# Another layout for the pairs' activations, a merged last read, and SwiGLU at once in pairs 10 and 11

## The chip, the cores and the metric

One core of one Trainium2 chip runs the kernel. The metric is the device time of that core in microseconds. Five engines share an on-chip memory (SBUF): TensorE (PE; its weight loads are shown as PEld), VectorE (DVE), ScalarE (ACT), GpSimd (POOL) and SyncE (SP), which issues the transfers. TensorE writes into eight banks of 128x512 floats (PSUM).

## What is computed

A transformer block over 512 tokens of width 2048, all in float32: a projection, two attentions, gates and an output projection, cross attention, and then the part of interest here, which the reference writes as

```python
def swiglu(h, w_gu, w_down):
    g, u = jnp.split(h @ w_gu, 2, axis=-1)
    return (jax.nn.silu(g) * u) @ w_down
...
hf = rmsnorm(x, norm_ffn_g[l])
x = x + swiglu(hf, w_gu[l], w_down[l])
```

with 5632 hidden features, that is 44 tiles of 128. A final norm follows.

## The kernel before

Activations are kept transposed: 16 tiles (k) of 128 features by 512 tokens. For accuracy each float is split in two parts, a high one (rounded to the type that TensorE multiplies) and the low rest, and a product is high x high + high x low + low x high. ScalarE makes the high part of a piece of weights (`convert`, `mix_convert`, lines 597 and 946), VectorE subtracts it from the raw one to make the low part (`units`, `mix_low`, lines 1093 and 1580), TensorE uses both. Weights stream in pieces called units.

Of the 44 hidden tiles two (DIRECT) are computed plainly, by `panel` in `ffn_first` and behind it (lines 2159 to 2237). The other 42 make 21 **pairs**, each with a gate product and an up product of two tiles: 42 groups g, and group 2p-2 is the gate of pair p, 2p-1 its up. A group is computed with seven block products for eight (Strassen's scheme in Winograd's form, `PRODUCTS`, line 132): blocks of the features' halves by the tokens' halves. Three of the products ("b") read the activations themselves (blocks B11, B21 and B22), four ("t") read sums prepared in `t_both`. GpSimd makes the sums of the weights (lines 564 to 571). A group has four units c; in each of them every product gets four matmuls: two wide ones, high weights by low and high activations beside each other (128x512, line 2175), and two narrow ones, low weights by high activations (128x256, line 2178). Each group leaves seven banks: product 0 in one of two acc banks, by turns, the others in six that all groups share.

VectorE reads a group's banks in `read_products` (line 1597) while TensorE works on the group's last unit and on the next group's first. The reading is told by semaphore of products 0, 2, 4 and 5 (`TOLD`) and of the unit's end, and frees banks in four steps (`READ_STEPS`, `FREED_BY`), for which TensorE waits before the next group's products 1, 3, 5 and 6. Every addition waits for the one before. Between two readings VectorE makes four low parts. ScalarE can make the high part of unit n once unit n-3 is done (line 951).

For pairs 1 and 2 (`INLINE`) SwiGLU is done at once: VectorE scales the gate product by the norm's factor `rstd`, ScalarE takes the sigmoid, VectorE multiplies twice, and after the up product once more; the result is stored to `gate_t`. For the other pairs gate and up product are stored to memory, and are fetched, scaled and multiplied in the down stage. There the rows of w_down run in `ORDER`, with 11 groups of four hidden tiles. The first of them needs the two inline pairs, for nothing is left to do on them but the split.

The **seam** is the passage from pairs to down stage. SyncE fetches the first weights of the down stage, then per unit a part of x, and once, at c == 1, both pairs of tiles of `hidden_in(0)` (lines 487 to 498). ScalarE and VectorE split them, VectorE before it reads the last group (lines 1716 to 1729). TensorE starts on the down stage when both are split; its two acc banks come free when VectorE has added the first ones to x (`add_out`, line 1453; `down`, line 1669). SBUF space is shared: `over` (fetched tiles, and two of four places for the raw weights of pairs, `mix_raw`) and `act_both` lie on the same bytes.

## Time and profile before

| | |
|---|---|
| median of 3 runs | 2774.85 us (2771.26 to 2776.34) |
| profiled execution, its own time | 2777.86 us |
| its span, first to last instruction | 2776.1 us |
| mean granted clock of TensorE | 0.994 |
| busy: PE / PEld / DVE / ACT / POOL | 98% / 82% / 63% / 37% / 27% |
| stage of the pairs | 1413.6 to 2269.4 us |
| down stage, with its end | 2269.6 to 2776 us |

The rows show one execution. PE is busy from a matmul's start to its modelled end, and matmuls overlap, so the time that TensorE loses is read from the distance of starts and from the waits. "L1585" is line 1585 of the kernel. The arrow "<-" in a wait names what released it. A wide matmul of two separate runs of 256 and one of a single run of 512 have the same shape in a row, 128x512.

### The profile page before, as it was taken

How to read it: one execution, taken by the hardware profiler on the slowest of the kernel's cores; microseconds unless marked ns; L12 is line 12 of the kernel's file. 1: busy time of each engine (PE TensorE's matmuls, PEld its weight loads, DVE VectorE, ACT ScalarE, POOL GpSimd, SP SyncE). 2: the span in 40 equal slices, each digit the busy share in tenths (PEclk: the TensorE clock that was granted, in tenths of full speed). 3: DMA queues.
4: the chain of work that ended last, by engine and by line, in shares of the span. 5: the costliest groups of instructions: out<-in, count | busy, mean ns of one | idle time of the engine just before them, and what ended most of it. 6: DMA issues, size and time to landing. Idle time of an engine off the chain costs nothing.

```text
span 2776.1 us, 35075 instructions
## 1 busy us (share of the span) xinstructions
PE 2720.1 (98%) x13710; PEld 2285.9 (82%) x13710; DVE 1742.1 (63%) x1904; ACT 1018.1 (37%) x1134; POOL 742.4 (27%) x642
## 2 busy tenths in 40 slices
PE   9999999999999999999998999999999999999997
PEld 7888888888788888887777888888888878888886
DVE  6677643345643343674677767777777767777786
ACT  6545532224642231243643333333333332222224
POOL 0000000000000003420366566665656532222120
PEclk9999999999999999999999999999999999999999
DMA  6222233232223334333333343434343464434432
GB/s 239 73 91 68 68 103 98 91 99 85 79 82 97 98 119 165 95 117 104 129 112 104 127 138 128 137 123 143 122 142 124 138 231 132 154 132 153 158 123 84
DMA packets 125890, 333.30 MB, mean 120 GB/s; under 512 B 10320, under 2 KB 57424, under 8 KB 125136
## 3 DMA queue, kind: packets, MB, share of 16 engines
q1 hardware_dynamic: 119296, 309.37, 34.4%
q10 hardware_dynamic: 6480, 22.35, 2.0%
q8 instruction: 79, 1.29, 0.2%
q14 instruction: 35, 0.29, 0.0%
HBM read 301.27 MB, written 30.41 MB: 119 GB/s over the span
## 4 chain that ended last, share of the span: by engine, by line
PE 80%; DVE 14%; ACT 2%; issue 1%; DMA 1%; POOL 1%; SPq 0%; DVEq 0%; ACTq 0%
PE acc L1803 14%; PE acc L1805 14%; PE acc L1804 14%; PE ps L2175 9%; PE acc L1830 6%; PE acc L1831 6%; PE acc L1832 6%; PE ps L2178 5%; PE acc L2175 2%; DVE w_lo L1585 2%; DVE cg L1612 2%; DVE cg L1613 2%; DVE cu L1613 2%; DVE cu L1612 2%; DVE wm_lo L1585 1%
## 5 line engine op out<-in xcount | busy, mean ns | idle before, releaser
L1098 DVE TENSOR_TENSOR w_lo<-raw,w_hi 128x1024 fp32r<-128x1024 f32 x328 | 476.6, 1457 | 282.9 <-ACT w_hi L607 282.3
L1803 PE MATMUL acc<-act_both,w_hi 128*128 128x512 f32 (+1 forms) x1536 | 590.9, 385 | 1.3 <-DVE sq_sum L1490 1.0
L1805 PE MATMUL acc<-act_both,w_lo 128*128 128x512 f32 (+1 forms) x1536 | 584.9, 381 | 0.0
L1804 PE MATMUL acc<-act_both,w_hi 128*128 128x512 f32 (+1 forms) x1536 | 584.7, 381 | 0.0
L607 ACT ACTIVATE w_hi<-raw 128x1024 fp32r<-128x1024 f32 x328 | 344.6, 1055 | 565.6 <-PE acc L1805 339.2
L1803 PEld LDWEIGHTS acc<-act_both,w_hi 128*128 128x128 f32 x1536 | 289.2, 188 | 57.0 <-DVE sq_sum L1490 1.5
L1805 PEld LDWEIGHTS acc<-act_both,w_lo 128*128 128x128 f32 x1536 | 289.1, 188 | 55.6
L1804 PEld LDWEIGHTS acc<-act_both,w_hi 128*128 128x128 f32 x1536 | 289.3, 188 | 54.6 <-issue 0.7
L2175 PE MATMUL ps<-t_both,w_hi 128*128 128x512 f32 x896 | 282.6, 397 | 0.1
L541 POOL MEMSET mem_stat<- 128x256 f32 x1 | 0.3, 312 | 1049.2 <-DMA mem<-mem_t 1049.2
L1830 PE MATMUL acc<-act_both,w_hi 128*128 128x512 f32 x672 | 263.5, 392 | 4.3 <-DVE x L1453 4.0
L1831 PE MATMUL acc<-act_both,w_hi 128*128 128x512 f32 x672 | 262.4, 390 | 0.0
L1832 PE MATMUL acc<-act_both,w_lo 128*128 128x512 f32 x672 | 262.1, 390 | 0.0
L1453 DVE TENSOR_TENSOR x<-x,acc 128x512 f32<-128x512 f32 (+1 forms) x216 | 147.5, 683 | 140.3 <-PE acc L1832 86.7
L2178 PEld LDWEIGHTS ps<-t_both,w_lo 128*128 128x128 f32 x896 | 168.9, 188 | 40.0
L1585 DVE TENSOR_TENSOR w_lo<-raw,w_hi 128x1792 fp32r<-128x1792 f32 x56 | 121.4, 2168 | 87.9 <-ACT w_hi L952 87.0
L2178 PE MATMUL ps<-t_both,w_lo 128*128 128x256 f32 x896 | 176.5, 278 | 0.0
L952 ACT ACTIVATE w_hi<-raw 128x1792 fp32r<-128x1792 f32 x56 | 95.4, 1703 | 192.8 <-PE ps L2178 179.1
L952 ACT ACTIVATE w_hi<-over 128x1792 fp32r<-128x1792 f32 x56 | 95.6, 1706 | 172.9 <-PE ps L2178 162.1
L569 POOL TENSOR_TENSOR over<-over 128x512 f32<-128x512 f32 x84 | 155.1, 1846 | 6.6
L1830 PEld LDWEIGHTS acc<-act_both,w_hi 128*128 128x128 f32 x672 | 126.4, 188 | 34.7 <-DVE w_lo L1098 4.1
L1832 PEld LDWEIGHTS acc<-act_both,w_lo 128*128 128x128 f32 x672 | 126.6, 188 | 26.6
(300 smaller groups left out, 4718.9 us busy)
## 6 DMA issues: line engine op xcount, KB each, us to landing
raw<-w_stream SPq DMA_DIRECT2D x412, 512.0 KB, 3.6
over<-w_stream SPq DMA_DIRECT2D x84, 512.0 KB, 4.7
gate_t<-cg ACTq DMA_DIRECT2D x22, 512.0 KB, 2.6
over<-gate_t SPq DMA_DIRECT2D x22, 512.0 KB, 5.4
up_t<-cu ACTq DMA_DIRECT2D x20, 512.0 KB, 2.6
over<-up_t SPq DMA_DIRECT2D x20, 512.0 KB, 6.2
x<-x_t SPq DMA_DIRECT2D x16, 512.0 KB, 8.9
x_tokens<-x_n SPq DMA_DIRECT2D x4, 1024.0 KB, 15.4
```

The lines of the kernel that those rows point to most:

```text
L607: nc.scalar.activation(w_hi[:, s, :], raw[:, s, :], ACT.Copy).then_inc(hi_done, 1)
L952: nc.scalar.activation(mix_half(True, i), mix_raw(i)[:, 1:8, :], ACT.Copy).then_inc(hi_done, 1)
L1098: nc.vector.tensor_tensor(w_lo[:, s, :], raw[:, s, :], f(w_hi[:, s, :]), ALU.subtract)\
L1585: nc.vector.tensor_tensor(mix_half(False, i), mix_raw(i)[:, 1:8, :], f(mix_half(True, i)), ALU.subtract).then_inc(lo_done, 1)
L1803: nc.tensor.matmul(dst, wh, ah, start=start and k == 0, stop=False)
L1804: nc.tensor.matmul(dst, wh, al, start=False, stop=False)
L1805: last = nc.tensor.matmul(dst, wl, ah, start=False, stop=stop and k == UK - 1)
L1830: nc.tensor.matmul(dst[n], wh, ah, start=k == 0, stop=False)
L1831: nc.tensor.matmul(dst[n], wh, al, start=False, stop=False)
L1832: last = nc.tensor.matmul(dst[n], wl, ah, start=False, stop=k == GROUP - 1)
L2175: nc.tensor.matmul(dst, hi[:, w_block, P * j:P * (j + 1)], src[:, :, ks.start + 2 * c + j, toks], start=c == 0 and j == 0, stop=False)
L2178: last = nc.tensor.matmul(dst[:, SH:S], lo[:, w_block, P * j:P * (j + 1)], src[:, 1, ks.start + 2 * c + j, toks], start=False, stop=c == 3 ...
```

## The change

- The activations for the direct panels and the pairs lie in `act_mix`, by tile k, half of the tokens, low or high part, 256 tokens. The low and the high part of one block stand beside each other, and a wide matmul of a "b" product reads 512 floats in one run. A direct panel reads the two halves of a tile's tokens, 256 each, from two places. The "t" products are unchanged. Hidden tiles of the down stage lie in `late`, by tile, then low or high; `over` likewise, so two fetched tiles are no longer in one run.
- The six shared banks are numbered in a row. `read_products` reads products 5 and 6 together, with two additions over two banks once the unit is done; three steps and three tellings remain.
- `INLINE` is 10, 11 and `ORDER` starts with them. In these pairs the third multiplication of the gate (by `rstd`) is moved behind the up product, and the multiplications there lie behind one low part each. The numbers of the waits for stored products follow from `UPS_STORED`. ScalarE's order in the pairs is as it was.
- The seam: the first fetched pair of tiles is asked for at c == 0, the second at c == 1, each with a semaphore of its own. ScalarE's high part of the second pair of tiles moves behind a high part of weights; VectorE's split of the first moves ahead of a low part, and the low part between the last reading and the first addition to x moves behind that addition.

The diff, cut to its core (left out: declarations, the passing of `x_low` a view, renamings from act to late, the waits' numbers on ScalarE):

```diff
@@ -132,13 +132,14 @@
-READ_STEPS = 4
-FREED_BY = {1: 1, 3: 2, 5: 3, 6: 4}
-TOLD = (0, 2, 4, 5)
...
-INLINE = 2
-ORDER = [*range(1, MIXES + 1), 0]
+READ_STEPS = 3
+FREED_BY = {1: 1, 3: 2, 5: 3}
+TOLD = (0, 2, 4)
...
+INLINE = 10, 11
+ORDER = [*INLINE, *(p for p in range(1, MIXES + 1) if p not in INLINE), 0]
+UPS_STORED = [1 + sum(q not in INLINE for q in range(1, p + 1)) for p in range(MIXES + 1)]
@@ -193,10 +194,16 @@
         with ExitStack() as a:
-            over = sb("over", [P, 2, KT, S], F32, a)
+            over = sb("over", [P, KT, 2, S], F32, a)
+        with ExitStack() as a:
+            act_mix = sb("act_mix", [P, KT, 2, 2, SH], F32R, a)
+        with ExitStack() as a:
+            late = sb("late", [P, KT, 2, S], F32R, a)
         act_both = sb("act_both", [P, 2, KT, S], F32R)
         act_lo, act_hi = (act_both[:, n, :, :] for n in range(2))
-        over_lo, over_hi = (over[:, n, :, :] for n in range(2))
+        over_lo, over_hi = (over[:, :, n, :] for n in range(2))
+        mix_lo, mix_hi = (act_mix[:, :, :, n, :] for n in range(2))
+        late_lo, late_hi = (late[:, :, n, :] for n in range(2))
         raw = sb("raw", [P, RING, UK * P], F32)
@@ -266,7 +273,8 @@
         acc = [ctx.enter_context(nc.psum_tensor(f"acc{n}", [P, S], F32)) for n in range(2)]
-        ps = [ctx.enter_context(nc.psum_tensor(f"ps{n}", [P, 3 * S], F32)) for n in range(2)]
+        both_ps = ctx.enter_context(nc.psum_tensor("ps", [P, 6 * S], F32))
+        ps = [both_ps[:, 3 * S * n:3 * S * (n + 1)] for n in range(2)]
@@ -351,14 +362,17 @@
         def hid_tile(slot, k):
-            return act_tile(UK + GROUP * slot + k)
...
+            return late_hi[:, UK + GROUP * slot + k, :], late_lo[:, UK + GROUP * slot + k, :]
...
+        def halves(tile):
+            return tile.rearrange("p (t c) -> p t c", t=2)
...
             if n % 4 >= 2:
-                return (over_lo, over_hi)[n % 4 - 2][:, 0:UK, SH:S]
+                return over[:, 0:UK, 1, SH * (n % 4 - 2):SH * (n % 4 - 1)]
             return raw[:, 2 * (n % 4):2 * (n % 4) + 2, :].rearrange("p r (b c) -> p (r b) c", b=4)
@@ -378,11 +392,10 @@
                 return acc[n][:]
-            t, b = ((0, 0), (0, 1), (1, 0), (1, 1), (0, 2), (1, 2))[i - 1]
-            return ps[t][:, S * b:S * (b + 1)]
+            return both_ps[:, S * (i - 1):S * i]
         def two_banks(t, h):
-            return ps[t][:, 0:2 * S].rearrange("p (a s) -> p a s", a=2)[:, :, SH * h:SH * (h + 1)]
+            return both_ps[:, 2 * S * t:2 * S * (t + 1)].rearrange("p (a s) -> p a s", a=2)[:, :, SH * h:SH * (h + 1)]
@@ -466,14 +479,14 @@
-            def hidden_in(g):
...
-                for b in range(0, GROUP, 2):
+            def hidden_in(g, parts=range(0, GROUP, 2)):
...
+                for b in parts:
                     p = ORDER[2 * g + b // 2]
                     sp.wait_ge(gate_stored, 16 * (p + 1))
-                    sp.dma_start(over_lo[:, hid_part(g % 2, b), :], gate_t[p, :, :, :]).then_inc(hid_in[g % 2], 16)
+                    sp.dma_start(over_lo[:, hid_part(g % 2, b), :], gate_t[p, :, :, :]).then_inc(hid_in[g % 2] if g else hid_in_first[b // 2], 16)
                     if g:
-                        sp.wait_ge(up_stored, 16 * (p - INLINE + 1 if p else 1))
+                        sp.wait_ge(up_stored, 16 * UPS_STORED[p])
                         sp.dma_start(over_hi[:, hid_part(g % 2, b), :], up_t[p, :, :, :]).then_inc(hid_in[g % 2], 16)
@@ -489,8 +502,8 @@
                 sp.wait_ge(unit_done, U_DOWN - 3 + c)
-                if c == 1:
-                    hidden_in(0)
+                if c < 2:
+                    hidden_in(0, [2 * c])
                 x_in_again(c)
@@ -926,7 +939,9 @@
                 for m in (2 * n, 2 * n + 1):
-                    x_high(act_hi[:, m, :], m, G_FFN)
+                    read_out()
+                    nc.scalar.activation(mix_hi[:, m, :, :], halves(x[:, m, :]), ACT.Copy,
+                                         scale=par[:, G_FFN + m:G_FFN + m + 1]).then_inc(h_hi, 1)
                     if m > 1:
@@ -1017,17 +1032,18 @@
                     mix_convert()
-                    convert(1)
-                    act.wait_ge(hid_in[0], 32)
                     for b in range(0, GROUP, 2):
-                        nc.scalar.activation(act_hi[:, hid_part(0, b), :], over_lo[:, hid_part(0, b), :], ACT.Copy)\
+                        if b:
+                            convert(1)
+                        act.wait_ge(hid_in_first[b // 2], 16)
+                        nc.scalar.activation(late_hi[:, hid_part(0, b), :], over_lo[:, hid_part(0, b), :], ACT.Copy)\
                             .then_inc(hid_hi, 1)
...
                 if inline:
-                    act.wait_ge(hid_made, p)
+                    act.wait_ge(hid_made, INLINE.index(p) + 1)
                     store_gate(p)
@@ -1622,10 +1638,8 @@
                 between()
-                dve.wait_ge(products_done, len(TOLD) * g + 4)
-                added(out[:, 1, :], out[:, 1, :], lambda h: half(5, h), freed)
                 dve.wait_ge(unit_done, U_MIX + 4 * (g + 1))
-                added(out[:, 2, :], out[:, 2, :], lambda h: half(6, h), freed)
+                added(out[:, 1:3, :], out[:, 1:3, :], lambda h: two_banks(2, h), freed)
@@ -1700,32 +1714,33 @@
             rstd_of(4, rstd, S)
             mix_low(4)
             for p in range(1, MIXES + 1):
-                inline, last = p <= INLINE, p == MIXES
+                inline, last = p in INLINE, p == MIXES
                 dve.wait_ge(gate_stored, 16 * p)
                 read_products(2 * p - 2, cg)
                 mix_low()
                 if inline:
-                    dve.wait_ge(up_stored, 16)
+                    dve.wait_ge(up_stored, 16 * UPS_STORED[p - 1])
                     nc.vector.tensor_tensor(cg[:], cg[:], both, ALU.mult).then_inc(gate_scaled, 1)
                 mix_low()
                 if inline:
-                    dve.wait_ge(sig_made, p)
+                    dve.wait_ge(sig_made, INLINE.index(p) + 1)
                     link(nc.vector.tensor_tensor(cg[:], cg[:], cu[:], ALU.mult))
-                    link(nc.vector.tensor_tensor(cg[:], cg[:], both, ALU.mult))
                 mix_low()
                 if last:
+                    hidden_low(0, 0)
                     units()
-                    hidden_low(0, 0)
                     hidden_low(0, 2)
                 else:
                     mix_low()
-                dve.wait_ge(up_stored, 16 * (max(0, p - INLINE - 1) + 1))
+                dve.wait_ge(up_stored, 16 * UPS_STORED[p - 1])
                 read_products(2 * p - 1, cu, units if last else lambda: None)
                 if inline:
-                    nc.vector.tensor_tensor(cg[:], cg[:], cu[:], ALU.mult).then_inc(hid_made, 1)
-                if last:
-                    units()
-                else:
+                    mix_low()
+                    link(nc.vector.tensor_tensor(cg[:], cg[:], cu[:], ALU.mult))
+                    mix_low()
+                    nc.vector.tensor_tensor(cg[:], cg[:], both, ALU.mult).then_inc(hid_made, 1)
+                    mix_low(2)
+                elif not last:
                     mix_low(4)
             unit.add(MIX_UNITS * MIXES)
@@ -1748,9 +1763,9 @@
                 for n in range(KT // 2):
-                    down(2 * n, first=first, between=lambda: next_group(n))
...
-            arrived = Tally(32), Tally()
+                    down(2 * n, first=first, between=units if first and n == 0 else lambda: next_group(n))
...
+            arrived = Tally(), Tally()
             per_group = [(converted, KT), (unit, KT), (out_no, 2 * KT), (half, KT), (hid, GROUP), (arrived[0], 64),
@@ -2170,14 +2185,16 @@
                         pe.wait_ge(products_read, READ_STEPS * (g - 1) + FREED_BY[at])
-                    src = act_both if kind == "b" else t_both
+                    if kind == "b":
+                        src = [act_mix[:, ks.start + 2 * c + j, toks.start // SH, :, :] for j in range(2)]
+                    else:
+                        src = [t_both[:, :, ks.start + 2 * c + j, toks] for j in range(2)]
                     for j in range(2):
-                        nc.tensor.matmul(dst, hi[:, w_block, P * j:P * (j + 1)], src[:, :, ks.start + 2 * c + j, toks],
-                                         start=c == 0 and j == 0, stop=False)
+                        nc.tensor.matmul(dst, hi[:, w_block, P * j:P * (j + 1)], src[j], start=c == 0 and j == 0,
+                                         stop=False)
                     for j in range(2):
-                        last = nc.tensor.matmul(dst[:, SH:S], lo[:, w_block, P * j:P * (j + 1)],
-                                                src[:, 1, ks.start + 2 * c + j, toks], start=False,
-                                                stop=c == 3 and j == 1)
+                        last = nc.tensor.matmul(dst[:, SH:S], lo[:, w_block, P * j:P * (j + 1)], src[j][:, 1, :],
+                                                start=False, stop=c == 3 and j == 1)
                     if c == 3 and at in TOLD:
```

## Rows read from the trace of the kernel before

**Rows 1.** Busy times of a stretch: start:end; length, PE, PEld, DVE, ACT, POOL, clock, DMA.

```profile
1413.40:2269.50 856.10, 836.22 (x4706) 721.46 (x4704) 613.57 (x671) 289.65 (x173) 539.88 (x498) 0.99 0.41 132
```

**Rows 2.** Timeline of TensorE, steady group: start us, us, what, count.

```profile
1699.71 0.63 PE L2175 MATMUL acc<-act_both,wm_hi 128*128 128x512 f32 x2
...
1700.41 0.63 PE L2175 MATMUL ps<-act_both,wm_hi 128*128 128x512 f32 x2
...
1704.59 0.63 PE L2175 MATMUL acc<-act_both,w_hi 128*128 128x512 f32 x2
```

**Rows 3.** Waits of weight loads, 1532.9 to 2253 us: total, times, longest.

```profile
PEld acc L2175 <- DVE w_lo L1585: 9.7, 24, 0.7
PEld acc L2175 <- DVE wm_lo L1585: 5.1, 12, 0.9
```

**Rows 4.** Waits of matmuls, 1413.5 to 1532.9 us: total, times, longest.

```profile
PE acc L2175 <- DVE wm_lo L1585: 6.1, 3, 2.8
PE acc L2175 <- DVE w_lo L1585: 6.0, 4, 3.4
```

**Rows 5.** Busy times of a stretch behind a long wait, with its granted clock.

```profile
1511.30:1518.10 6.80, 5.40 (x17) 4.63 (x18) 5.22 (x3) 1.04 (x1) 1.69 (x2) 0.50 0.62 215
```

**Rows 6.** Timeline of VectorE, one reading of a steady group.

```profile
2007.08 0.69 DVE L1612 TENSOR_TENSOR cg<-ps,cg 128x512 f32<-128x512 f32 x1 [0.51 <-PE ps L2178]
2007.81 0.69 DVE L1613 TENSOR_TENSOR cg<-ps,cg 128x512 f32<-128x512 f32 x1
...
2010.90 0.42 DVE L1612 TENSOR_TENSOR cg<-ps,cg 128x256 f32<-128x256 f32 x1
...
2012.73 2.02 DVE L1585 TENSOR_TENSOR wm_lo<-raw,wm_hi 128x1792 fp32r<-128x1792 f32 x1
```

**Rows 7.** Timeline of TensorE at the unit that follows that reading.

```profile
2014.24 0.40 PE L2178 MATMUL ps<-t_both,w_lo 128*128 128x256 f32 x2
2014.81 0.74 PE L2175 MATMUL acc<-act_both,wm_hi 128*128 128x512 f32 x2 [0.17 <-DVE wm_lo L1585]
```

**Rows 8.** Timeline of VectorE and ScalarE, gate product of pair 2.

```profile
1484.85 2.02 DVE L1585 TENSOR_TENSOR w_lo<-raw,w_hi 128x1792 fp32r<-128x1792 f32 x1
...
1486.80 1.22 DVE L1709 TENSOR_TENSOR cg<-cg,rstd 128x1024 f32<-128x1024 f32 x1
...
1488.05 1.06 ACT L1013 ACTIVATE cu<-cg 128x1024 f32<-128x1024 f32 x1 [9.24 <-DVE cg L1709]
...
1490.73 2.41 DVE L1585 TENSOR_TENSOR w_lo<-over,w_hi 128x1792 fp32r<-128x1792 f32 x1 [2.72 <-ACT w_hi L952]
...
1493.07 2.31 DVE L1713 TENSOR_TENSOR cg<-cg,cu 128x1024 f32<-128x1024 f32 x1
```

**Rows 9.** Timeline of TensorE, down stage: whole tiles, then the halves of its end.

```profile
2725.93 0.39 PE L1830 MATMUL acc<-act_both,w_hi 128*128 128x512 f32 x1
...
2727.97 0.39 PE L1830 MATMUL acc<-act_both,w_hi 128*128 128x512 f32 x1
...
2739.79 0.28 PE L2227 MATMUL acc<-act_both,w_hi 128*128 128x256 f32 x1
...
2740.03 0.28 PE L2229 MATMUL acc<-act_both,w_lo 128*128 128x256 f32 x1
```

**Rows 10.** Timeline of SyncE queue, ScalarE and VectorE at the seam.

```profile
2259.74 1.49 SPq L474 DMA_DIRECT2D over<-gate_t  x2
...
2266.11 2.01 ACT L1023 ACTIVATE act_both<-over 128x1024 fp32r<-128x1024 f32 x2 [0.36 <-DMA over<-gate_t]
...
2269.47 0.42 DVE L1617 COPY cu<-acc 128x256 f32<-128x256 f32 x1
...
2277.17 1.23 DVE L1098 TENSOR_TENSOR w_lo<-raw,w_hi 128x1024 fp32r<-128x1024 f32 x1
```

**Rows 11.** Timeline of TensorE at the seam.

```profile
2275.00 0.39 PE L1832 MATMUL acc<-act_both,w_lo 128*128 128x512 f32 x1
2279.14 0.64 PE L1830 MATMUL acc<-act_both,w_hi 128*128 128x512 f32 x1 [3.75 <-DVE x L1453]
```

34 lines of the change are left out of this document (18 added, 16 removed).

## Prediction

> **What bounds the kernel now.** The page comes first: TensorE is busy for 98% of the span and VectorE for 63%, so a change can pay in two ways only, by making TensorE's own work shorter or by closing its gaps. Next I cut the span by stage. The stage of the pairs (lines 2164 to 2191, 168 units of 28 matmuls) lasts 856 us and TensorE is busy for 836 of them [rows 1], but "busy" counts a matmul from start to modelled end and these overlap, so idle time is read better from the starts. With no wait, one unit begins 4.88 us after the last (1699.71 to 1704.59), one product 0.70 us after the last [rows 2]. 168 x 4.877 = 819.3 us. The stage takes 855.8 from first start to last, so 36.5 us of it are waits and their after-effects. The rest of the prediction is mainly about these.
>
> They fall in two heaps. In the 36 steady groups the weight loads wait 9.7 + 5.1 = 14.8 us, always for the low halves of the weights (line 1585), 0.41 a group [rows 3]. In the first five groups, where SwiGLU is done at once for pairs 1 and 2, TensorE's matmuls wait 12.1 us in seven places [rows 4], and two stretches at half clock follow the long ones, 3.4 us and 6.8 us at 0.50; the second is shown [rows 5]. From the unit starts, the groups with pairs 1 and 2 lose 18.7 us against 4.877 a unit, of which 4.3 is time at the lower clock.
>
> **Part 1, the reading.** For one group VectorE reads seven products (lines 1616 to 1628) and only then makes the next low half. In a steady group the reading ends at 2012.73; its last four additions of 128x256 take 2012.73 - 2010.90 = 1.83 us, 0.46 each, while one addition over two banks comes 2007.81 - 2007.08 = 0.73 after the other [rows 6]. The change makes two of the second kind out of the four: 1.46 us for 1.83, and the low half begins 0.38 us sooner, with 0.69 us of work each and the same link between them. It removes one wait (fourth "products_done") and keeps the wait for the whole unit; that one is met long before, since the group's last unit, 4.88 us long, starts at 2004.72 and ends near 2009.6, and the two additions begin at 2010.90 [rows 6]. The next low half ends at 2014.75, the load of its weights starts after it, and the matmul comes at 2014.81; without a wait the load would have come just after the previous unit's last matmul (second of the two that begin at 2014.24, so 2014.36) [rows 6, 7]. Hence 0.45 us lost now. With 0.38 less, 0.07 stays, and about 0.02 more since TensorE gets a little quicker (part 3): 0.09. For 37 groups (all but the first and the four with SwiGLU in them) 37 x 0.36 = 13.3 us. Who waits for the merged step: TensorE's product 5 of the next group writes a bank that is freed by it, and comes 5 x 0.70 = 3.5 us into its unit, at 2013.1; the step ends at 2012.35. No new wait, with 0.7 us to spare. Should it cost what four took, the gain is 0; should the whole wait vanish, 37 x 0.45 = 16.6.
>
> **Part 2, SwiGLU in pairs 10 and 11 for pairs 1 and 2.** What is removed at the start: 18.7 us. What stays there: in group 0 the reading starts late (VectorE had to catch up with the first weights), and its first unit after the reading waits 1.27 us for matmuls, 1.78 by the starts, of which 0.38 goes by part 1; I leave 1.5 us. What is added in the middle is read from pair 2, the one nearest to a steady start. Gate product: low half (1484.85), times rstd (1486.80, 1.22 us), sigmoid on ScalarE (1488.05, 1.06), then ScalarE's next high half, and only then VectorE's next low half at 1490.73, which took 2.41 [rows 8]. This queue is not changed: ScalarE still waits with its high half behind the sigmoid. So one wait stays, 1.1 in matmul idle and 1.4 by the starts; part 1 takes 0.38 of it, the pair lands a little later against a unit without loss: 1.0 to 1.7 us, I take 1.3. What is gone: the third multiplication ahead of the third low half (1.65 us, which cost the wait of 0.8), and the one ahead of the low half after the odd reading, which cost 3.4 us and the half clock behind it. They lie now behind two low halves each. VectorE has room: a group needs 6.3 us of reading and 4 x 2.0 of low halves out of 19.5, so 5.2 are free, against two multiplications of 1.2 (alone) to 2.3 us (2.31 at 1493.07, beside GpSimd) [rows 8]. After the odd reading ScalarE's last two high halves wait for the product, as they did; by the order it is there some 14 us into the group and the low half at 18.3, needed at 19.5; if both multiplications take 2.3 it is late by 1 us. So 2 x 1.3 = 2.6 us, bounds 2 and 8. Sum of part 2: 18.7 - 1.5 - 2.6 = 14.6; the two groups of each new pair keep 0.09 of part 1 as well, -0.4: 14.2.
>
> The Trainium skill ("SBUF — State Buffer", Who interferes with whom) says that a VectorE instruction with two SBUF inputs contends with GpSimd's reads. The trace agrees: 2.31 us for a multiplication beside GpSimd's work, 1.22 without.
>
> **Part 3, the layout.** A wide matmul on the pairs reads two runs of 256 that lie far apart, two of them span 0.63 us, so 0.63 - 0.40 = 0.233 from start to start [rows 2]; on one run of 512 it is (2727.97 - 2725.93)/9 = 0.227 [rows 9]. Three of seven products change: 168 x 3 = 504 of them, two wide matmuls each. A whole product takes 0.697. Made of contiguous prices, 2 x 0.227 + 2 x 0.120 (narrow ones in a row, 2739.79 to 2740.03 [rows 9]) = 0.694: 3 ns less, 1.5 us in all. If instead the narrow ones keep what they have now, it is 12 ns less, 6.3 us. I take 2.0, nearer to the first end, since each product is as long as its four matmuls at their own prices. Against it: the four direct panels (192 wide matmuls of line 1803 to 1805) now read two runs: 192 x 6 ns = 1.2 us more. Net gain 0.8. ScalarE, VectorE and the transfers touch the same number of elements in other strides; I cost this at nothing, because these engines are waited for at the places named here only, and price a few ns a matmul among the rivals.
>
> The skill ("SBUF — State Buffer", Door 1: The DMA port swizzle) has it that only a step beyond a 16-byte line costs; by that rule one jump in 512 elements is free, and the layout brings nothing (total 0.8 us worse than mine).
>
> **Part 4, the seam.** Now: both gate tiles of the first down group are fetched at 2259.74, ScalarE has them at 2266.11, VectorE splits both (1.15 each) and starts reading the last group at 2269.47, though its products were there from about 2265.3; the reading with one low half in it ends at 2277.17, another low half (1.15) follows, then the first addition to x (0.68); TensorE, with nothing free to write to, stands from 2275.2 to 2279.14, and then 3.4 us at half clock come [rows 10, 11]. After: tiles 0 and 1 are fetched a unit earlier, their split (done by about 2263.5) leaves the path; then low half (2265.8), second split, reading at 2268.2: 1.3 us sooner. It takes 4.7 + 1.2 (low half) + 1.45 = 7.35 for 7.7, and the second low half lies behind the addition to x: addition done at 2276.2, TensorE resumes at 2276.4. Stall 1.6 in place of 3.9 us, and no half clock after so short a one (behind the waits of 1.3 and 2.5 us the clock stayed at its upper level, behind those of 2.8 and 3.4 [rows 4] and this one it fell): 2.3 + 1.5 + 0.4 at the first down matmuls (they waited for the second split) = 4.2 us. Bounds 2.5 (half clock stays) and 5.
>
> **Sum.** 13.3 + 14.2 + 0.8 + 4.2 = 32.5 us. Profiled execution: 2777.9 - 32.5 = 2745.4; it is 3.0 above the median of the runs, 2774.85, so the time is 2742.4, said as 2742.5.
>
> **Rivals.** (a) The lower weights stay late: the merged additions over two banks save nothing, or the load that begins late costs a refill anyway (about 0.1 us after each wait is seen in the first matmul, 0.74 for two instead of 0.63 [rows 2, 7]). Then the 13.3 us stay: 2756. For it: 0.09 us of margin is computed from a difference of 0.07. Against: the chain of the reading is link by link and leaves no slack elsewhere. (b) SwiGLU costs in the middle what it cost at the start, because the loss comes from ScalarE's order, which stays: 2 x 9 - 2.6 = 15 us more, less the clock part if no stall is as long as those: 2753 to 2757. For it: the same wait of 1.4 us is kept. Against: two of the three long waits sat behind multiplications that are moved. (c) Contiguous reading pays fully, 2738. (d) Slower than before: the two halves lying together make TensorE's read, not its array, the limit for the 1008 wide matmuls of the b products, or for those of the down stage, say through other engines working in the same tile. Each ns on 1008 matmuls is 1.0 us. It decides from 33 ns a matmul (0.260 in place of 0.227); at 40 ns the time is 2782. Against: the largest effect of form in the trace is 6 ns. (e) The change does not do what it says: all of layout and merging bring nothing, and only the moved SwiGLU and the seam are left, 2757, as in (a).
>
> **Chances.** Forecast 0.64, (a) with (e) 0.13, (b) 0.12, (c) 0.08, (d) 0.03. Range: from 2733 (forecast with layout and refill at their best ends: 5 + 3 us, seam 1) to 2758 (a or b alone); both together, 2771, lie outside. About 0.2% (5.5 us) is what a measurement of this kernel can tell from no change: faster by more 0.95 (all but (d), less 0.02 for (a) and (b) at once and at their worst), within 0.02, slower by more 0.03.
>
> **What would show it.** Steady groups: weight loads wait under 0.15 us a group for line 1585's successor and units at 4.87 throughout; waits of the first two pairs down to one of 1 to 1.5 us; one stall of 1 to 1.7 us in each of groups 18 and 20 and no half clock near them; the b products shorter than the t products by 3 ns (or 12); the seam's stall near 1.6 us at full clock. Wrong would be: a half-clock stretch in the middle, waits of TensorE for products_read, b products no shorter, or a slower down stage (matmuls there more than 0.227 apart).

## The result, and the profile after

The changed kernel takes 2757.4 us (median of 4 runs, 2755.5 to 2758.8) where the kernel before took 2775.6 beside it: ratio 0.9937, 95% interval 0.9920 to 0.9954. That is 0.6% faster, 14.9 us more than the predicted 2742.5 and at the upper edge of the range (2758). The profiled execution took 2757.35 us (span 2755.6) against 2777.86: 20.5 us less, where the sum said 32.5. (The other 3 us of the miss are the distance by which the profiled execution of before lay above its median, which I took off; that of after lies on it.)

The page's busy times of after:

```profile
PE 2708.8 (98%) x13710; PEld 2282.3 (83%) x13710; DVE 1740.2 (63%) x1820; ACT 1019.7 (37%) x1134; POOL 768.4 (28%) x642
```

The stretch of the pairs, from the first to the last matmul, answering [rows 1]:

```profile
1413.30:2247.20 833.90, 824.86 (x4706) 718.11 (x4705) 615.05 (x591) 289.59 (x173) 564.85 (x498) 1.00 0.42 135
```

The waits of matmuls at the start (1413.3 to 1510 us), answering [rows 4]:

```profile
PE acc L2193 <- DVE wm_lo L1601: 0.7, 1, 0.7
PE acc L2193 <- DVE w_lo L1601: 0.5, 1, 0.5
```

The waits of weight loads between 1510 and 1770 us and, second line, between 1885 and 2250 us, answering [rows 3]:

```profile
PEld acc L2193 <- DVE wm_lo L1601: 0.5, 1, 0.5
...
PEld acc L2193 <- DVE w_lo L1601: 0.4, 1, 0.4
```

The stage of the pairs is 22 us shorter and its granted clock is 1.00. The waits of weight loads in the steady groups, 14.8 us before, are 0.9 in the two stretches shown; those of the first five groups, 12.1 us, are 1.2, with no stretch at the lower clock behind them. (These views list no wait under 0.15 us; by the starts of the units 0.07 us a steady group is left.) What is new stands in the middle, pairs 10 and 11 (waits of matmuls, 1770 to 1885 us):

```profile
PE acc L2193 <- DVE w_lo L1601: 3.9, 3, 2.4
PE acc L2193 <- DVE wm_lo L1601: 3.5, 3, 1.3
```

By the starts of the units, as in the prediction (excess over 4.877 us a unit; "start" is the first five groups, "middle" groups 18 to 23, "rest" the other 31), the two profiled executions compare so:

| | before | predicted change | measured change | after |
|---|---|---|---|---|
| first pair matmul at | 1413.63 | +1.2 | -0.25 | 1413.38 |
| units' own time, 168 x 4.877 | 819.3 | -2.0 | 0.0 | 819.3 |
| start | 18.7 | -16.8 | -16.6 | 2.2 |
| middle | 2.65 | +0.5 | +6.6 | 9.2 |
| rest | 14.95 | -11.2 | -11.8 | 3.1 |
| behind the last pair matmul | 506.9 | -4.2 | +1.6 | 508.5 |
| sum | | -32.5 | -20.5 | |

(The predicted -27.5 of parts 1 and 2 is shared out over start, middle and rest by its own steps: 0.36 a group, 18.7 to 1.5, and 2.6 for the two new pairs.) Three lines missed: the middle by 6, the seam by 6, the layout's units by 2. The experiments are about these three, and about which part of the change earned what.

### The profile page after: what moved, and what is told of

Same layout as the page of the kernel before. It is cut to its first block, busy times and chain, and to the rows that moved or that the text cites. A ratio compares the mean times of both kernels' runs of the same rounds, so it can differ in the third digit from the quotient of the medians.

```text
span 2755.6 us, 34949 instructions
## 1 busy us (share of the span) xinstructions
PE 2708.8 (98%) x13710; PEld 2282.3 (83%) x13710; DVE 1740.2 (63%) x1820; ACT 1019.7 (37%) x1134; POOL 768.4 (28%) x642
## 4 chain that ended last, share of the span: by engine, by line
PE 88%; DVE 6%; ACT 2%; issue 2%; DMA 1%; POOL 1%; SPq 0%; DVEq 0%; ACTq 0%
PE ps L2193 14%; PE acc L1818 14%; PE acc L1820 14%; PE acc L1819 14%; PE ps L2196 7%; PE acc L1845 5%; PE acc L1846 5%; PE acc L1847 5%; PE acc L2193 3%; PE acc L2196 1%; DVE w_lo L1601 1%; DMA x_tokens<-x_n 1%; PE ps L1887 1%; PE ps L1876 1%; DVE cg L1629 1%
## 5 line engine op out<-in xcount | busy, mean ns | idle before, releaser
L1818 PE MATMUL acc<-act_both,w_hi 128*128 128x512 f32 (+1 forms) x1472 | 565.4, 384 | 1.2 <-DVE sq_sum L1506 1.0
L1820 PE MATMUL acc<-act_both,w_lo 128*128 128x512 f32 (+1 forms) x1472 | 559.9, 380 | 0.0
L1819 PE MATMUL acc<-act_both,w_hi 128*128 128x512 f32 (+1 forms) x1472 | 559.5, 380 | 0.0
L1818 PEld LDWEIGHTS acc<-act_both,w_hi 128*128 128x128 f32 x1472 | 277.1, 188 | 54.4 <-DVE sq_sum L1506 1.5
L1820 PEld LDWEIGHTS acc<-act_both,w_lo 128*128 128x128 f32 x1472 | 276.9, 188 | 53.1
L1819 PEld LDWEIGHTS acc<-act_both,w_hi 128*128 128x128 f32 x1472 | 277.2, 188 | 51.7 <-issue 0.5
L1845 PE MATMUL acc<-late,w_hi 128*128 128x512 f32 x672 | 263.5, 392 | 5.8 <-DVE x L1469 5.8
L1846 PE MATMUL acc<-late,w_hi 128*128 128x512 f32 x672 | 262.4, 390 | 0.0
L1847 PE MATMUL acc<-late,w_lo 128*128 128x512 f32 x672 | 262.1, 390 | 0.0
L1845 PEld LDWEIGHTS acc<-late,w_hi 128*128 128x128 f32 x672 | 126.4, 188 | 36.6 <-DVE w_lo L1114 4.2
L1847 PEld LDWEIGHTS acc<-late,w_lo 128*128 128x128 f32 x672 | 126.6, 188 | 26.6
```

The costliest lines, as they stand in the source:

```text
L1818: nc.tensor.matmul(dst, wh, ah, start=start and k == 0, stop=False)
L1819: nc.tensor.matmul(dst, wh, al, start=False, stop=False)
L1820: last = nc.tensor.matmul(dst, wl, ah, start=False, stop=stop and k == UK - 1)
L1845: nc.tensor.matmul(dst[n], wh, ah, start=k == 0, stop=False)
L1846: nc.tensor.matmul(dst[n], wh, al, start=False, stop=False)
L1847: last = nc.tensor.matmul(dst[n], wl, ah, start=False, stop=k == GROUP - 1)
```

## Experiments

All were timed beside the kernel before. "Pairs" is the time from the first to the last pair matmul, "end" what lies behind it, both of the profiled execution. One trace's small differences need care: e9 and e11 below run the same instructions in the middle and lose 3.9 and 2.1 us there, and among e8, e9, e10 and e12, which are the same from the seam on, the end takes 505.9 to 506.6 us.

**e1, the layout alone** (kernel before, with `act_mix`, `late`, the new `over` and what reads them)

```diff
-            over = sb("over", [P, 2, KT, S], F32, a)
+            over = sb("over", [P, KT, 2, S], F32, a)
...
+            act_mix = sb("act_mix", [P, KT, 2, 2, SH], F32R, a)
...
+            late = sb("late", [P, KT, 2, S], F32R, a)
...
```

> Only the layout of act_mix, late and over changes. Prediction's theory (contiguous reads are quicker): products of the b kind 3 ns shorter, the direct panels' matmuls 6 ns longer, in all 0.8 us faster. Theory after the first trace (a wide matmul's 0.233 comes from narrow ones beside it, not from two runs): every product stays 0.697 us, panels stay 0.227 a matmul, stage of the pairs 855 to 856 us; fetches into over go in 2 KB pieces, 1.9 us each for 1.3, but the seam has slack for that: 0 to +1.5 us in all.

2777.3 us, ratio 1.0011 (1.0002 to 1.0021): a little slower, not faster, and 1 us more than the second theory allowed. A unit without a wait takes 4.877 us as before. The pairs are 2.9 us shorter than before, but 2.9 of that is the start, which in this execution had one stretch of half clock fewer; the end is 3.0 us longer.

**e2, the merged reading alone**

```diff
-READ_STEPS = 4
+READ_STEPS = 3
...
-                added(out[:, 1, :], out[:, 1, :], lambda h: half(5, h), freed)
-                added(out[:, 2, :], out[:, 2, :], lambda h: half(6, h), freed)
+                added(out[:, 1:3, :], out[:, 1:3, :], lambda h: two_banks(2, h), freed)
```

> Only the last two products are read together. My theory: the low half after each reading comes 0.38 us sooner, weight loads wait 0.07 a group for 0.44, in all 41 groups 14 to 16 us faster, stage of the pairs about 840 us. Rival (the refill of the weights is paid anyway): 0.1 or more stays besides, 10 us or less.

2756.4 us, ratio 0.9936 (0.9919 to 0.9952): this one edit gives all that the whole change gives. Pairs 835.2 us, 20.4 less: 12.5 in the rest, 2.2 in the middle (together 14.7 for 37 groups, 0.40 each), and 5.6 at the start, where in this execution no half clock follows the long waits. The waits of its matmuls in the first five groups, SwiGLU still in pairs 1 and 2, and of its weight loads in all later groups:

```profile
PE acc L2173 <- DVE w_lo L1585: 5.3, 4, 2.6
PE acc L2173 <- DVE wm_lo L1585: 4.9, 3, 2.8
```

```profile
PEld acc L2173 <- DVE wm_lo L1585: 0.3, 1, 0.3
```

The waits at the start are still 10.2 us, with longest ones of 2.6 and 2.8; the excess is 13.1 us instead of 18.7.

**e3, SwiGLU moved to pairs 10 and 11 alone** (the new `INLINE`, `ORDER`, `UPS_STORED` and the order of the multiplications)

> Only pairs 10 and 11 instead of 1 and 2 get SwiGLU at once, with the multiplications in their new places. Prediction's theory: the start gains 17 us, the middle costs 2 x 1.3: 14 us faster. Theory after the first trace: the middle costs about 9 to 11 us, since VectorE comes late to the next reading and its low half after it runs beside GpSimd (2.6 to 2.9 us for 2.0): 4 to 8 us faster, no half clock in the pairs.

2769.1 us, ratio 0.9981 (0.9971 to 0.9991). The start falls from 18.7 to 3.6 us, the middle rises from 2.65 to 9.8: half of the gain is given back. The second theory holds (4 to 8 us, no half clock), the prediction's 14 us does not.

**e4, the seam's order alone**

```diff
-                if c == 1:
-                    hidden_in(0)
+                if c < 2:
+                    hidden_in(0, [2 * c])
...
-                    units()
                     hidden_low(0, 0)
+                    units()
                     hidden_low(0, 2)
```

> Only the seam's order changes, layout as before (4 KB pieces). Theory of the 2 KB pieces: the weights of the down stage's fifth unit land about 11 us after the last pair's matmul, not 13.4; the stall before the third unit is about 1.7 us for 4.0; in all 1.5 to 4.5 us faster than before. Rival (the order itself moves the wait from the first to the second place whatever the pieces): stall of 4 us there and half clock behind it, +1 us or no change.

2774.3 us, ratio 0.9998 (0.9988 to 1.0007): nothing. The long stall is gone, and with it the half clock, but TensorE now stands three times (its matmuls that waited at the seam):

```profile
2275.51 0.47 PE L1829 MATMUL acc<-act_both,w_hi 128*128 128x512 f32 x1 [1.68 <-DVE x L1454]
2282.36 0.47 PE L1829 MATMUL acc<-act_both,w_hi 128*128 128x512 f32 x1 [1.16 <-DVE x L1454]
2289.96 0.47 PE L1829 MATMUL acc<-act_both,w_hi 128*128 128x512 f32 x1 [1.90 <-DVE x L1454]
```

The first is the 1.6 us that was predicted. The two others are new: each time VectorE is held up by a low part of weights that has to be fetched first. Of the expected theory the landing of the weights holds (11.1 us) and the gain doesn't; of the rival only "no change" does, for there is no stall of 4 us and no half clock.

**e5, the changed kernel with the down stage's weights asked for first**

```diff
-            hidden_in(1)
             late_weights(4)
-            for c in range(4, 8):
-                x_in_again(c)
+            hidden_in(1, [0])
+            late_weights(5)
+            hidden_in(1, [2])
+            late_weights(6)
+            x_in_again(4)
+            late_weights(7)
+            x_in_again(5)
...
```

> The changed kernel, but in the seam SyncE asks for the weights of the down stage's units 4 to 7 ahead of or between the fetches of hidden tiles and x, not behind them. Theory (the seam is bound by the transfer queue, in the order in which it is asked): the stall of 4.2 us before the third unit and the half clock behind it go, the time behind the last pair's matmul falls from 508.5 to 502 to 504 us, 5 to 6 us faster than the changed kernel. Rival (VectorE's order of low parts and additions is what binds): no more than 1 us.

2754.6 us, ratio 0.9926 (0.9909 to 0.9942), the intervals overlap with those of the changed kernel (2757.4). The weights of unit 4 come in time, and the stall of 3.84 us in matmul idle becomes two of 1.7, behind the first one, which is as it was:

```profile
2261.51 0.50 PE L1851 MATMUL acc<-late,w_hi 128*128 128x512 f32 x1 [1.73 <-DVE x L1475]
2266.25 0.47 PE L1851 MATMUL acc<-late,w_hi 128*128 128x512 f32 x1 [1.73 <-DVE x L1475]
```

Now VectorE waits for the hidden tiles of the next group, which were moved back (idle for 3.82 us until they land). The end stays at 508.5 us, so the theory's 502 to 504 is refuted: bringing the weights forward is not enough.

**e6, the changed kernel with ScalarE's next high half ahead of the sigmoid**

```diff
-                mix_convert()
+                mix_convert(2)
                 if inline:
                     act.wait_ge(gate_scaled, INLINE.index(p) + 1)
                     nc.scalar.activation(cu[:], cg[:], ACT.Sigmoid).then_inc(sig_made, 1)
-                mix_convert()
```

> The changed kernel, but ScalarE makes the second high half of an inline pair ahead of the sigmoid, not behind it. Theory (the wait of 1.35 us in the gate group is ScalarE's order, and VectorE's lateness in the next groups starts from it too): the two waits of 1.3 us and part of the four behind them go, pairs 10 and 11 cost 3 to 5 us in place of 9.2. Rival (the loss is VectorE's own load of multiplications beside GpSimd, whatever ScalarE does): 7 us or more stay.

2752.2 us, ratio 0.9919 (0.9903 to 0.9936), 5.2 below the changed kernel (the intervals overlap); the middle falls from 9.2 to 4.6 us. VectorE and ScalarE in the first gate product of e6:

```profile
1791.95 2.02 DVE L1600 TENSOR_TENSOR wm_lo<-over,wm_hi 128x1792 fp32r<-128x1792 f32 x1
```

```profile
1792.06 1.06 ACT L1028 ACTIVATE cu<-cg 128x1024 f32<-128x1024 f32 x1 [3.98 <-DVE cg L1722]
```

The low half starts straight behind the multiplication (1790.81, 1.22 us), while the sigmoid runs.

**e7, wide matmuls first, narrow ones behind them** (changed kernel; in the first three units of each group, since the fourth has to end product by product. The expectation below speaks of the two middle units; what ran reorders one unit more, c = 0, and that one decides the time.)

```diff
-                    for j in range(2):
-                        last = nc.tensor.matmul(dst[:, SH:S], lo[...], src[j][:, 1, :], ...)
+                    if c < 3:
+                        srcs[at] = (w_block, dst, src)
...
+                for at, args in srcs.items():
+                    last = narrow(at, *args)
```

> The changed kernel, but in the two middle units of each group all 14 wide matmuls come first, then all 14 narrow ones. Theory (0.233 and 0.115 are the prices of wide and narrow matmuls beside each other, 0.227 and 0.120 those in a row of one width, whatever the runs): wide matmuls of those units 0.227 apart, narrow 0.120, a unit 4.86 us for 4.877, 1 to 2 us faster. Rival (the pairs' operands or addresses cost it): wide matmuls stay 0.233.

2774.3 us, ratio 0.9998 (0.9989 to 1.0008). The timeline of TensorE in a unit of e7, and its waits for VectorE's reading between 1533 and 2240 us:

```profile
1704.67 0.62 PE L2201 MATMUL ps<-act_mix,w_hi 128*128 128x512 f32 x2
1705.13 1.53 PE L2201 MATMUL ps<-t_both,w_hi 128*128 128x512 f32 x6
1706.49 0.62 PE L2201 MATMUL ps<-act_mix,w_hi 128*128 128x512 f32 x2
...
1707.87 0.88 PE L2188 MATMUL ps<-t_both,w_lo 128*128 128x256 f32 x6
1708.59 0.40 PE L2188 MATMUL ps<-act_mix,w_lo 128*128 128x256 f32 x2
```

```profile
PE ps L2201 <- DVE cu L1629: 5.2, 19, 0.4
PE ps L2201 <- DVE cg L1629: 5.0, 18, 0.6
```

Six wide matmuls on `t_both`, two distant runs of 256 each, take 1706.49 - 1705.13 = 1.36 us, 0.227 apiece; the two on `act_mix`, one run of 512, take 0.46, 0.23 each, the same within the rows' hundredths. The narrow ones take 0.72 / 6 = 0.120. So the distances of 0.233 and 0.115 in [rows 2] belong to wide and narrow matmuls by turns, not to the layout: 7 x 4 matmuls take 4.873 us in one order and 4.877 in the other. The time is lost at c = 0: product 5's bank is written 2.3 us into the unit there instead of 3.5 (1706.49 against 1704.20), before the merged step has freed it, and the unit takes 5.48 us. So the expected distances are there, and the expected gain of 1 to 2 us is not.

**e8, all of the change but the layout**

> The changed kernel without its layout: merged read, moved SwiGLU and the seam's order only. Theory (the layout gives TensorE nothing and costs the seam transfers of 2 KB pieces): the pairs take 833 to 834 us as in the changed kernel, and the time behind their last matmul falls by 2 us, fetches into over take 1.3 us each for 1.8; 2 us faster than the changed kernel. Prediction's theory: 1.5 to 2 us slower in the pairs, 1.2 faster in the panels.

2755.9 us, ratio 0.9930 (0.9913 to 0.9946). Pairs 833.5 us, as with the layout (833.7); the end is 506.4, 2.1 less. At the seam it has stalls of 1.27, 1.70 and 1.60 us in matmul idle and no half clock.

**e9, e8 with both waits of ScalarE eased**: the sigmoid as in e6, and one more high half ahead of the store

```diff
                 else:
-                    mix_convert(4)
+                    mix_convert(5 if inline else 4)
                 if inline:
                     act.wait_ge(hid_made, INLINE.index(p) + 1)
                     store_gate(p)
...
-                    mix_convert(2)
+                    mix_convert(1 if inline else 2)
```

> The changed kernel without its layout, with two edits of ScalarE's order in pairs 10 and 11: the high half that stood behind the sigmoid goes ahead of it (as in e6), and one of the two high halves behind the store of the product goes ahead of that store. Theory (ScalarE's queue causes the stalls): the all-but-layout kernel stood at 2755.9; the sigmoid edit gave 4.5 us in the middle (9.2 to 4.55), and the store edit should take most of the stall of 1.34 us between the first two units of groups 21 and the like of it in 19, since VectorE waited 2.20 us for that high half before the reading: middle 3.0 to 3.8, pairs 827.0 to 828.5, the end as in e8 (506.4), time 2749 to 2751. Rival (VectorE is short of time whatever the order, because GpSimd slows it): the middle stays at 4.5 or above and the time at 2751.5 or above.

2747.7 us, ratio 0.9898 (0.9882 to 0.9915): below both kernels. The middle is 3.9 us; against e6 two stalls moved, those of the first units of groups 21 and 23 (1.34 to 0.97 and 1.22 to 0.98), which together is less than e9 and e11 differ by. The rest of the distance to e6 is in the end, which is 4.1 us shorter. What is left in the middle is of one kind. VectorE starts the readings of groups 19 to 22 0.97 us into their last unit, as in a steady group, but the low halves behind them take 2.49, 3.04, 3.05 and 3.05 us for 2.02; the first of them:

```profile
1808.76 2.49 DVE L1586 TENSOR_TENSOR wm_lo<-raw,wm_hi 128x1792 fp32r<-128x1792 f32 x1
```

**e10, e9 with the old order of the multiplications** (two behind the sigmoid, the last straight behind the up product's reading)

> e9 with the multiplications of pairs 10 and 11 in the order of the kernel before: two behind the sigmoid in the gate, the last straight behind the up product's reading. Theory of my prediction: the reordering is what takes the two long stalls away, so without it each of the two pairs costs 3 us or more beyond e9, stalls near 3 us come back behind the odd reading, perhaps with half clock: middle 9 to 13, time 2756 to 2760. Rival: with ScalarE's high halves ahead, the order of the multiplications matters little (VectorE does the same work in a group): middle within 1.5 us of e9, time 2750 to 2752.

2752.7 us, ratio 0.9918 (0.9901 to 0.9934). The middle is 5.05 us for 3.9, nearly all of it in two stalls (waits of matmuls of e10, 1770 to 1885 us):

```profile
PE acc L2172 <- DVE w_lo L1586: 2.1, 1, 2.1
PE acc L2172 <- DVE wm_lo L1586: 2.1, 1, 2.1
```

In e9 the same waits are four, 2.7 us together, none over 0.8. No half clock followed in e10 either. The profiled executions (2749.2 and 2749.7 us) agree with the rival; the medians, 5.0 us apart, lie between it and the theory of the prediction, and their intervals overlap: the order of the multiplications is worth 1 to 5 us for both pairs together, not the 9 and more that were hung on it.

**e11, e9 with the queue of e5**

> e9 with the order of e5 in the transfer queue at the seam: the raw weights of the down stage's units 4 to 7 are asked for ahead of the later hidden tiles and parts of x. With the fetches in pieces of 4 KB. Theory (the seam is bound by the sum of the transfers, not by their order): stalls of 1.7, 2 and 2 us, the stage behind the pairs within 1 us of e9's. Rival (what counts is when the weights of unit 4 land): the second stall of 2.1 us goes, and the end is 1.5 to 2.5 us shorter than e9's.

2746.0 us, ratio 0.9894 (0.9878 to 0.9911), the fastest version that computes everything, though not apart from e9. Its end is 0.8 us shorter, as the theory has it (within 1 us); but the second stall is nearly gone, as the rival has it, and a later one takes its place, with stalls again in three places, the first of 1.28 us and these two:

```profile
2254.66 0.50 PE L1836 MATMUL acc<-act_both,w_hi 128*128 128x512 f32 x1 [0.52 <-DVE x L1460]
2259.41 0.47 PE L1836 MATMUL acc<-act_both,w_hi 128*128 128x512 f32 x1 [1.74 <-DVE x L1460]
```

**e12, e9 with GpSimd's sums over 32 of 256 columns in pairs 10 and 11** (that part of the sums is left out)

```diff
-                part = mix_raw(n)
+                part = mix_raw(n)[:, :, 0:32 if 70 <= n < 90 else 2 * P]
...
```

> e9 with GpSimd's sums of the weights made over 32 of 256 columns in the units of pairs 10 and 11 (units 70 to 89), so part of the computation there is left out. Theory: what is left in the middle comes from VectorE's low halves and multiplications beside GpSimd (2.4 to 2.9 for 2.02 us, 1.75 to 2.3 for 1.22): the low half behind each reading takes 2.02, each stall of 1.2 to 1.3 us there falls to 0.5 to 0.7, the middle to 1.0 to 2.2, the time 1.5 to 2.5 us below e9. Rival (ScalarE's wait and the sum of VectorE's own work decide): the middle falls by under 0.7 us.

2745.3 us, ratio 0.9893 (0.9876 to 0.9909); the middle is 1.0 us. The two instructions of VectorE behind the reading of group 19, in e12:

```profile
1808.71 2.03 DVE L1586 TENSOR_TENSOR wm_lo<-raw,wm_hi 128x1792 fp32r<-128x1792 f32 x1
1810.65 1.22 DVE L1724 TENSOR_TENSOR cg<-cg,cu 128x1024 f32<-128x1024 f32 x1
```

The same two took 2.49 and 1.75 us in e9, 2.93 and 1.75 in the changed kernel. The low halves behind the readings of groups 19 to 22 take 2.03, 2.02, 2.02 and 2.62 us in e12; three of the four stalls behind them are at the steady 0.07 us, and the fourth (0.55) stands behind the long one. In the time the effect (2.4 us) isn't apart from e9; in the durations it is.

## Why the prediction was right or wrong

**Part 1, right.** The steady reading of the changed kernel (timeline of VectorE, answering [rows 6]):

```profile
1993.56 0.69 DVE L1628 TENSOR_TENSOR cg<-ps,cg 128x512 f32<-128x512 f32 x1
1994.28 0.69 DVE L1629 TENSOR_TENSOR cg<-ps,cg 128x512 f32<-128x512 f32 x1
1995.01 2.03 DVE L1601 TENSOR_TENSOR wm_lo<-raw,wm_hi 128x1792 fp32r<-128x1792 f32 x1
```

The last two products take 1995.01 - 1993.56 = 1.45 us (predicted 1.46), and 0.07 us a group is left (predicted 0.09); the term was 13.3 and e2 measured 14.7. What I missed is that the same edit pays a second time, at the start: in e2 its groups lose 5.6 us less. About 1.4 of that is 4 x 0.36, the rest fits the 4.3 us of half clock, of which none came in e2's execution. That the shorter waits are the reason isn't shown: e1, whose waits there are the old ones, had one stretch of half clock fewer as well. I had booked all this under part 2. So the gains of parts 1 and 2 overlap; the sum didn't suffer (it named the start once), but each part's worth did: by the medians of e1 to e4 the four edits alone come to 22.1 us, together they gave 18.2.

**Part 2, the start right, the middle wrong.** 18.7 went to 2.2 as predicted (to 1.9). The middle costs 9.2 us for 3.1. The step that failed is "VectorE has room: a group needs 6.3 us of reading and 4 x 2.0 of low halves out of 19.5, so 5.2 are free". The timelines of VectorE, ScalarE and TensorE (only its matmuls that waited) of the changed kernel, from the end of group 18's reading on:

```profile
1792.34 1.22 DVE L1723 TENSOR_TENSOR cg<-cg,rstd 128x1024 f32<-128x1024 f32 x1
...
1796.27 2.42 DVE L1601 TENSOR_TENSOR wm_lo<-over,wm_hi 128x1792 fp32r<-128x1792 f32 x1 [2.72 <-ACT wm_hi L967]
1798.62 2.31 DVE L1727 TENSOR_TENSOR cg<-cg,cu 128x1024 f32<-128x1024 f32 x1
...
1805.81 0.41 DVE L1633 COPY cu<-acc 128x256 f32<-128x256 f32 x1
...
1811.98 2.93 DVE L1601 TENSOR_TENSOR wm_lo<-raw,wm_hi 128x1792 fp32r<-128x1792 f32 x1
1814.84 1.75 DVE L1739 TENSOR_TENSOR cg<-cg,cu 128x1024 f32<-128x1024 f32 x1
...
1821.98 2.47 DVE L1601 TENSOR_TENSOR w_lo<-over,w_hi 128x1792 fp32r<-128x1792 f32 x1 [2.20 <-ACT w_hi L967]
...
1840.26 3.13 DVE L1601 TENSOR_TENSOR w_lo<-over,w_hi 128x1792 fp32r<-128x1792 f32 x1 [2.72 <-ACT w_hi L967]
```

```profile
1793.59 1.06 ACT L1028 ACTIVATE cu<-cg 128x1024 f32<-128x1024 f32 x1 [8.85 <-DVE cg L1723]
1794.56 1.69 ACT L967 ACTIVATE wm_hi<-over 128x1792 fp32r<-128x1792 f32 x1
```

```profile
1798.75 0.73 PE L2193 MATMUL acc<-act_mix,wm_hi 128*128 128x512 f32 x2 [1.11 <-DVE wm_lo L1601]
1814.97 0.73 PE L2193 MATMUL acc<-act_mix,wm_hi 128*128 128x512 f32 x2 [1.30 <-DVE wm_lo L1601]
...
1843.45 0.74 PE L2193 MATMUL acc<-act_mix,w_hi 128*128 128x512 f32 x2 [2.37 <-DVE w_lo L1601]
```

The stall that I had priced is there, 1.11 us at 1798.75, for the reason given: VectorE waits 2.72 us for a high half that stands behind the sigmoid. But I ended the account with it. VectorE comes out of it late, and much of what follows runs beside GpSimd's sums: low halves take 2.4 to 3.1 us for 2.02, the multiplication 2.31 for 1.22. I had summed the group with 4 x 2.0, though [rows 8] held a low half of 2.41. At 1805.81 the reading starts 1.1 us later in its unit than in a steady group. It makes up 0.5 of that, for it finds its products ready (6.17 us to the low half for 6.66), and the low half behind it takes 0.9 more: 1.5 us late, the stall at 1814.97 (1.30 in matmul idle, 1.48 by the starts), in a unit for which I had priced nothing. Of the readings of groups 19 to 22 three start late like this and one on time, with low halves of 2.63 to 2.93 us behind them, and ScalarE's high half behind the store adds to it (VectorE idle 2.20 at 1821.98). The longest stall, 2.37 us at 1843.45, is the priced one of the second pair: there the low half that waits for ScalarE comes after a late reading and takes 3.13 itself. The two priced stalls fell in the second units of groups 19 and 21, not in groups 18 and 20. So rival (b) was half right: ScalarE's order, which stays, makes the loss, though without half clock. e6 and e12 took the two causes away in turn: with the high half ahead of the sigmoid 9.2 falls to 4.6, and without most of GpSimd's work e9's 3.9 (2.1 in e11) falls to 1.0. e9 shows that the second cause doesn't need the first: its readings start on time, and its low halves are long all the same. Why GpSimd's sums come beside them in these pairs and not in steady groups is open.

The Trainium skill ("SBUF — State Buffer", Who interferes with whom), cited in the prediction for a multiplication, holds for the low halves as well: 2.03 us in e12 against 2.49 for the same one in e9, which differs only in GpSimd's sums.

**Part 3, wrong in the step that read 0.233 as the price of two runs.** The steady group of after (timeline of TensorE, answering [rows 2]):

```profile
1699.14 0.63 PE L2193 MATMUL acc<-act_mix,w_hi 128*128 128x512 f32 x2
...
1699.84 0.62 PE L2193 MATMUL ps<-act_mix,w_hi 128*128 128x512 f32 x2
...
1700.53 0.63 PE L2193 MATMUL ps<-t_both,w_hi 128*128 128x512 f32 x2
...
1704.02 0.62 PE L2193 MATMUL acc<-act_mix,w_hi 128*128 128x512 f32 x2
```

A b product, now on one run, starts 0.69 to 0.70 us before the next, a t product on two runs likewise, the unit 4.88. Both ends of the bound (3 and 12 ns a product) lay beyond zero, and zero is what it was; e7 shows why. The cost that I had charged to the panels (1.2 us) did not come either: their matmuls start 0.227 us apart before and after. (The line "first pair matmul at" can't tell this: kernels that are the same up to there have it at 1412.0 to 1414.5.) I had compared matmuls in different company, a wide one between narrow ones and a wide one among its like, and put the difference down to the layout. The rule of the Trainium skill that was weighed there ("SBUF — State Buffer", Door 1: The DMA port swizzle) gave the right answer, and the trace agrees with it: 4.877 us a unit with either layout.

What the layout does cost was not in the sum at all: "the transfers touch the same number of elements in other strides; I cost this at nothing". A fetched pair of hidden tiles is no longer one piece of 4 KB on a partition but two of 2 KB. The transfers while the four hidden fetches of the seam land, in the kernel before (2274 to 2279 us) and after (2251.2 to 2258.3 us):

```profile
DMA packets 571, 2.08 MB, mean 415 GB/s; under 512 B 64, under 2 KB 64, under 8 KB 571
```

```profile
DMA packets 1073, 2.37 MB, mean 333 GB/s; under 512 B 69, under 2 KB 69, under 8 KB 1073
```

The rates are 415 and 333 GB/s, but not all of that is the size of the pieces. e1 has the same pieces with the old order of the seam; while its four fetches land (2269.1 to 2275.4 us):

```profile
DMA packets 1082, 2.32 MB, mean 369 GB/s; under 512 B 72, under 2 KB 72, under 8 KB 1081
```

Taken from the landing before them to the last one's, this stretch runs at 386 to 416 GB/s in eight executions with 4 KB pieces (before, e2, e3, e4, e8, e9, e10, e12) and at 328 to 369 in four with 2 KB (the changed kernel, e1, e6, e7). A packet (here one piece, on one partition) of 4096 B takes 159 ns at the median in all of them, one of 2048 B 84, twice which is 6% more; and a fetch of 512 KB that nothing disturbs lands 1.33 to 1.36 us behind the last one with 2 KB pieces, 1.28 with 4 KB. The rest lies in stretches in which single packets take far longer, up to 1.2 us; they occur with both sizes, but more of them fall into this time with the layout, and no run shows why. The Trainium skill ("DMA: Bandwidth & Descriptors", Why small descriptors are slow) puts the loss in a fixed overhead of about 3 cycles for each packet; worked out by that page (64 or 128 beats of 32 bytes and 3 cycles), an estimate, it would be 4.5% in a packet of 2 KB and 2.3% in one of 4 KB, so some 2% between them. The packets of the trace show 6%, so here the measurement decides.

**Part 4, wrong in what is late next.** The step that failed is "Stall 1.6 in place of 3.9 us, and no half clock", priced at 4.2 us: it followed only VectorE's reading, and asked of no transfer when it lands. The first stall is as predicted, 1.27 us in matmul idle, 1.66 by the starts. Then comes one that the sum did not have (TensorE, VectorE and ScalarE at the seam of after, and the stretch behind it with its granted clock of 0.72 in the column before the last two):

```profile
2254.13 0.47 PE L1845 MATMUL acc<-late,w_hi 128*128 128x512 f32 x1 [1.27 <-DVE x L1469]
2263.68 0.47 PE L1845 MATMUL acc<-late,w_hi 128*128 128x512 f32 x1 [3.84 <-DVE x L1469]
```

```profile
2261.71 1.23 DVE L1114 TENSOR_TENSOR w_lo<-raw,w_hi 128x1024 fp32r<-128x1024 f32 x1 [4.85 <-ACT w_hi L620]
```

```profile
2260.62 1.06 ACT L620 ACTIVATE w_hi<-raw 128x1024 fp32r<-128x1024 f32 x1 [5.65 <-DMA raw<-w_stream]
```

```profile
2264.00:2270.00 6.00, 6.00 (x21) 4.75 (x20) 3.13 (x5) 2.12 (x2) 2.38 (x1) 0.72 0.92 369
```

Read from the bottom: ScalarE idles 5.65 us for raw weights of the down stage's unit 4, VectorE 4.85 for their high part, and TensorE 3.84 for an addition to x that stands behind their low part on VectorE. The weights had been queued behind four hidden fetches. Before, they landed 11.0 us after the last pair matmul, and the stall of [rows 11] hid that, for it lasted until 10; e4 takes that stall away alone and loses as much waiting for transfers. In the changed kernel they land at 13.4 us, in e6 and e7 (the same transfers) at 12.7; with 4 KB pieces at 10.5 to 11.3 under either order, and in e1, with 2 KB pieces and the old order, at 11.4. e5 and e11 put them first, and the hidden tiles are late in their place: no order that was tried gives back more than 0.8 us (e11). That the sum of the transfers is the bound, whatever the order, fits this but was not tested by itself; e5's expectation had it otherwise. So the seam's edit was worth 0 by itself (e4), and with the layout's smaller pieces the end came out 1.6 us longer instead of 4.2 shorter. The end of every execution sorts by the layout and not by the seam's order: 505.8 to 506.9 us without the layout and with the old order (before, e2, e3), 505.9 to 506.6 with the new one (e4, e8, e9, e10, e12), and 508.5 to 509.9 with the layout under either order (the changed kernel, e1, e5, e6, e7); e11, with its own queue and no layout, has 505.1. Its price is about 3 us, and the 1.6 above is at the lower side of it by chance. Some 1 us of this price lies in the first 192 matmuls of the down stage; the rest is spread over the down stage and differs between executions. Whether all of it comes from the 42 smaller fetches was not separated and stays open.

**The rivals and the range.** None of (a), (c), (d), (e) happened. The time is that of (b), but only half through (b): 6 us from the middle, 6 from the seam, 2 from the layout, less 2 us that came out better (the line ahead of the pairs 1.4, steady groups 0.6), and 3 from the base (the profiled execution of before lay above its median). Three misses of one sign were treated as independent small bounds. The range's upper end was set by one rival alone; that the time lies 0.6 us inside it is luck, not a confirmation of the sum. Of the signs of being wrong one came: b products no shorter. Waits for products_read, half clock in the middle, and down-stage matmuls more than 0.227 apart did not.

## What to carry to other kernels

Follow a late engine until it has caught up: an operation that comes to run beside another engine's work gets longer (2.02 to 3.1 us here), and the stall comes back in units that were never touched. Before a stall at a passage is closed, list when each transfer behind it lands, because what was hidden by the stall is the next wait; and give a layout's DMA pieces a line of their own in the sum (here some 3 us, against a TensorE gain of nothing). Where an in-order chain is late by a little in every group, one merged step (e2) can be worth the whole rest of a change.

## What the hardware showed

- The distance between matmuls depends on the neighbours: wide and narrow by turns 0.233 and 0.115 us, among their like 0.227 and 0.120 (e7), the sum being the same. Two distant runs of 256 floats cost nothing against one run of 512.
- A DMA packet of 4096 B took 159 ns at the median, one of 2048 B 84. An undisturbed fetch of 512 KB landed 1.28 us behind the last in pieces of 4 KB, 1.33 to 1.36 in pieces of 2 KB; slower stretches came with both.
- VectorE's subtraction over 1792 columns took 2.02 us alone and up to 3.13 beside GpSimd's sums; GpSimd's own addition over 256 columns rose from 0.74 to 2.4 us beside it.
- The length of a stall alone does not tell whether half clock follows, so the prediction's sorting by length doesn't hold beyond its own trace. In the pairs those of 2.1 us (e10), of 2.6 and 2.8 (e2) and one of 2.9 (e1) were followed by none; those of 2.8 and 3.4 before [rows 4] were, and so was one of 2.4 in e7 (granted clock 0.57 from 1850 to 1854 us), while the like of it in the changed kernel, 2.37 us at 1843.45, was not. At the seam one of 3.84 was (0.72 over the 6 us behind it).
